# A chunked state-space scan: step sums as products of 18 rounded rows, part of VectorE's work given to ScalarE and GpSimd

## The reference, cut to what matters

```python
xdt = x * dt[..., None]
a_cum = jnp.cumsum(dt * a.reshape(G, R), axis=2)
seg = a_cum[:, :, :, None] - a_cum[:, :, None]
decay_ls = jnp.exp(jnp.where(causal, seg, -jnp.inf))
cb = jnp.einsum("bclgn,bcsgn->bclsg", cm, bm)
y_diag = jnp.einsum("bclsg,bclsgr,bcsgrp->bclgrp", cb, decay_ls, xdt)
decay_to_end = jnp.exp(a_cum[:, :, -1:] - a_cum)
states = jnp.einsum("bclgn,bclgr,bclgrp->bcgrpn", bm, decay_to_end, xdt)
chunk_decay = jnp.exp(a_cum[:, :, -1])
# h <- h * chunk_decay + states, chunk after chunk; y_off = C h exp(a_cum)
y = y_diag + y_off + x * d_skip
```

## Time and profile before

| | us |
|---|---|
| median of 3 runs | 2749.34 |
| lowest, highest | 2748.38, 2751.9 |
| the profiled execution, whole | 2747.44 |
| its span in the profile | 2745.6 |
| TensorE busy, share of the span | 2606.7, 95% |
| VectorE busy | 1770.6, 64% |
| GpSimd busy | 1586.4, 58% |
| ScalarE busy | 1311.5, 48% |

### The profile page before, as it was taken

How to read it: one execution, slowest core, us unless ns; L and a number is a source line. 1 busy time by engine, 2 the same in 40 slices (tenths; PEclk the granted TensorE clock), 3 DMA queues, 4 the chain that set the end, 5 groups by cost and what they waited for, 6 DMA issues and landing times. The chain is left out here.

```text
span 2745.6 us, 41086 instructions
## 1 busy us (share of the span) xinstructions
PE 2606.7 (95%) x14122; PEld 1834.4 (67%) x14122; DVE 1770.6 (64%) x2152; ACT 1311.5 (48%) x2072; POOL 1586.4 (58%) x1222
## 2 busy tenths in 40 slices
PE   5999999989999999799989999999999999599998
PEld 3788777767888888566645555555555555388887
DVE  5532565644214554299969888898888889555554
ACT  4433333434333333211158777787778777322221
POOL 5876666688777777478746565665666666000000
PEclk7999999999999999899979999999999999799999
DMA  2543323323333323244541212303122111333231
GB/s 104 154 157 111 124 86 132 116 89 129 128 123 138 123 99 132 70 115 131 148 135 55 71 49 61 93 24 93 55 62 78 40 40 58 123 119 107 76 113 40
DMA packets 202405, 267.95 MB, mean 98 GB/s; under 512 B 12833, under 2 KB 136033, under 8 KB 195569
## 3 DMA queue, kind: packets, MB, share of 16 engines
q1 hardware_dynamic: 202224, 265.64, 30.4%
HBM read 168.84 MB, written 96.76 MB: 97 GB/s over the span
## 5 line engine op out<-in xcount | busy, mean ns | idle before, releaser
L1969 POOL TENSOR_TENSOR a_w<-a_beta,a_rest 128x1024 f32<-128x1024 f32 (+2 forms) x320 | 560.3, 1751 | 354.0 <-DVE a_rest L1926 207.3
L763 POOL TENSOR_TENSOR f_l_lo<-f_wst,f_l_hi 128x512 fp32r<-128x512 f32 x312 | 405.0, 1301 | 269.1 <-ACT f_l_hi L631 268.8
L1926 DVE TENSOR_TENSOR_SCAN a_rest<-a_keep,a_rest,a_ones 128x513 f32<-128x513 f32 x384 | 470.0, 1262 | 10.8 <-ACT a_keep L1896 10.8
L1846 PE MATMUL a_turn<-a_ident,a_w 128*128 128x128 f32 (+1 forms) x2432 | 342.9, 279 | 7.3 <-DVE a_wt L1880 6.1
L1861 PE MATMUL a_o<-a_wt,a_v 128*64 128x512 f32 (+3 forms) x1408 | 339.4, 560 | 8.9 <-DVE a_out L1936 8.9
L499 PE MATMUL f_xz<-f_t_hi,f_l_hi 128*128 128x512 f32 x832 | 330.2, 397 | 6.9 <-issue 4.4
L499 PE MATMUL f_xz<-f_t_hi,f_l_lo 128*128 128x512 f32 x832 | 326.3, 392 | 0.0
L499 PE MATMUL f_xz<-f_t_lo,f_l_hi 128*128 128x512 f32 x832 | 326.0, 392 | 0.0
L1880 ACT COPY a_wt<-a_turn 128x512 f32<-128x512 f32 (+3 forms) x440 | 225.1, 528 | 207.0 <-PE a_turn L1846 205.5
L1846 PEld LDWEIGHTS a_turn<-a_ident,a_w 128*128 128x128 f32 (+1 forms) x2432 | 256.7, 140 | 91.5 <-issue 65.8
L1896 ACT ACTIVATE a_keep<-a_z 128x1024 f32<-128x1024 f32 (+4 forms) x352 | 300.1, 852 | 4.6 <-PE a_z L1829 4.5
(11 more groups left out here) (242 smaller groups left out, 4472.7 us busy)
## 6 DMA issues: line engine op xcount, KB each, us to landing
f_wst<-in_w_pairs SPq DMA_DIRECT2D x52, 1024.0 KB, 5.5
scratch_gate<-f_out SPq DMA_DIRECT2D x64, 256.0 KB, 2.2
o_g<-scratch_mixed SPq DMA_DIRECT2D x32, 512.0 KB, 5.5
s_xc<-scratch_xbc SPq DMA_DIRECT2D x16, 768.0 KB, 5.3
scratch_xbc<-f_out SPq DMA_DIRECT2D x36, 256.0 KB, 2.1
scratch_q_hi<-f_out SPq DMA_DIRECT2D x32, 256.0 KB, 3.5
scratch_q_lo<-f_out SPq DMA_DIRECT2D x32, 256.0 KB, 3.6
scratch_v<-f_out SPq DMA_DIRECT2D x32, 256.0 KB, 2.3
```

The source lines that it names most:

```text
L763: return nc.gpsimd.tensor_tensor(out, a, b, op).then_inc(done, 1)
L1846: mm = nc.tensor.transpose(turn[h][0:rows, qi * P:(qi + 1) * P], tile[:, h, x:x + rows], ident[:, :])
L1926: mm = nc.vector.tensor_tensor_scan(rest[r % RS][:, h, tn - 1::-1], top, ones[:, 0:1].to_broadcast([P, tn]), start, ALU.mult, ALU.min)
L1969: nc.gpsimd.tensor_tensor(w[r % AS][:, :, 0:tn], beta[r % KEEPS][:, :, 0:tn], rest[r % RS][:, :, 1:tn + 1], ALU.mult).then_inc(w_ready, 1)
```

## The change

The running sums of the decay steps are computed once, in `scan_start`: for each of the 16 chunks and 16 heads the sum up to each frame, split into a rounded high part and a rounded rest, stored to a new scratch array `cum`. The differences of two running sums are then a product over 18 rows: 16 rows hold minus the sums against ones at the place of the head (`own`), 2 rows hold ones against the sums. The rows come by three small DMAs for each unit (`load_spans`: 8 KB, and twice 4 KB), the operands are float32r. ScalarE takes `Relu` of minus the difference and then `Exp` of minus that, two passes over 128x1024 in place of one; the triangle of ones is no longer needed there. The exponentials of the three sums for all chunks (`sums`) are computed once in `scan_start`. GpSimd no longer makes `ua`; it makes `xde` (`to_end`) and fades the state (`fade`), which VectorE did. VectorE's `xdt` now waits for `xde` of two units before, its addition to the state for GpSimd's `fade`. SyncE issues the six span loads of a chunk ahead of the store of its group 0. In `scan_start` SyncE issues the stores of `cum` ahead of `scan.loads`, for which it waits for the sums, and twelve span loads behind them.

```diff
+SPANS = 2 * HPG + 2
...
+        self.sums = self.sbuf("s_sums", [P, 3, NT, HEADS])
+        self.lag = [[self.sbuf(f"s_lag{s}{g}", [SPANS, P], F32R) for g in range(GROUPS)] for s in range(2)]
+        self.rise = [[self.sbuf(f"s_rise{s}{g}", [SPANS, HPG, P], F32R) for g in range(GROUPS)] for s in range(2)]
+        self.rise_loaded = [self.sems(f"s_rise_loaded{s}", GROUPS) for s in range(2)]
...
+    def load_spans(self, sp, s, g, i):
+        steps = self.scratch["cum"][:, bass.ds(i * 2 + s, 1), g * HPG:(g + 1) * HPG, :]
+        sp.dma_start(self.rise[s][g][SPANS - 2:SPANS, :, :].bitcast(F32),
+                     steps.rearrange("q o h l -> q (o h) l")).then_inc(self.rise_loaded[s][g], 16)
+        for q in range(2):
+            sp.dma_start(self.lag[s][g][q * HPG:(q + 1) * HPG, :].bitcast(F32),
+                         steps[q, :, :, :].rearrange("o h l -> (o h) l")).then_inc(self.rise_loaded[s][g], 16)
...
+            sp.wait_ge(cum_high, START + 2)
+            sp.wait_ge(cum_low, START + 2)
+            for q in range(2):
+                for b in range(2):
+                    sp.dma_start(scratch["cum"][q, b * (NT // 2):(b + 1) * (NT // 2), :, :].rearrange("t h l -> (t h) l"),
+                                 by_step[q][b][:, :].bitcast(F32)).then_inc(cum_stored, 16)
             scan.loads(sp)
+            sp.wait_ge(lag_ones, START + 2 * GROUPS)
+            sp.wait_ge(own_kept, START + 2 * GROUPS)
+            sp.wait_ge(cum_stored, START + 64)
+            for s in range(2):
+                for g in range(GROUPS):
+                    scan.load_spans(sp, s, g, 0)
...
+            scan.constants(pool)
+            nc.gpsimd.memset(own[:, :, :], 0.0).then_inc(own_step, 1)
+            for q in range(2):
+                pool.wait_ge(own_step, START + q + 1)
+                nc.gpsimd.affine_select(out=own[:, :, :], in_=own[:, :, :], compare_op=ALU.not_equal, fill=-1.0,
+                                        base=-q * HPG, pattern=[[-1, HPG], [0, P]], channel_multiplier=1).then_inc(own_step, 1)
...
+            pe.wait_ge(scan.made, 4)
+            pe.wait_ge(steps_ready, START + 1)
+            for b in range(2):
+                last = nc.tensor.matmul(ps[:, b, 0:P],
+                                        steps[:, b * (NT // 2):(b + 1) * (NT // 2), :].rearrange("p t h -> p (t h)"),
+                                        scan.upper[:, :], start=True, stop=True)
+            last.then_inc(cum_done, 1)
+            for q, lhs in enumerate((scan.upper, scan.later, scan.ones)):
+                last = nc.tensor.matmul(psums[:, q, :], lhs[:, :], steps[:, :, :].rearrange("p t h -> p (t h)"),
+                                        start=True, stop=True)
+            last.then_inc(sums_done, 1)
...
+            act.wait_ge(cum_done, START + 1)
+            for b in range(2):
+                nc.scalar.activation(by_step[0][b][:, :], ps[:, b, 0:P], ACT.Copy).then_inc(cum_high, 1)
+            act.wait_ge(sums_done, START + 1)
+            nc.scalar.activation(scan.sums[:, :, :, :].rearrange("p q t h -> p q (t h)"), psums[:, 0:3, :],
+                                 ACT.Exp).then_inc(sums_ready, 1)
+            act.wait_ge(own_step, START + 3)
+            for s in range(2):
+                for g in range(GROUPS):
+                    nc.scalar.activation(scan.rise[s][g][0:2 * HPG, :, :], own[:, :, :], ACT.Copy).then_inc(own_kept, 1)
...
+            nc.vector.tensor_copy(steps[:, :, :], dt_tok[:, 1:NT + 1, 1, :]).then_inc(steps_ready, 1)
+            for s in range(2):
+                for g in range(GROUPS):
+                    nc.vector.memset(scan.lag[s][g][:, :].bitcast(F32), 1.0).then_inc(lag_ones, 1)
+            for b in range(2):
+                dve.wait_ge(cum_high, START + b + 1)
+                nc.vector.tensor_tensor(by_step[1][b][:, :], ps[:, b, 0:P], by_step[0][b][:, :].bitcast(F32),
+                                        ALU.subtract).then_inc(cum_low, 1)
...
+                    if more:
+                        for g in range(GROUPS):
+                            sp.wait_ge(seg_ready[s][g], i + 1 + START)
+                            scan.load_spans(sp, s, g, i + 1)
...
-            def spread_steps(s, g, i):
-
-                pool.wait_ge(seg_ready[1 - s][g], i + s + START)
-                nc.gpsimd.tensor_tensor(ua[g][:, :, :], upper[:, :].unsqueeze(1).to_broadcast([P, HPG, P]),
-                                        over_heads(dt_of(i, s, 1, g), P), ALU.mult).then_inc(ua_ready[s][g], 1)
+            def to_end(s, g, i):
+
+                hs = slice(g * HPG, (g + 1) * HPG)
+                pool.wait_ge(xdt_ready[s][g], i + 1 + START)
+                pool.wait_ge(st_done[1 - s][g], i + s + START)
+                nc.gpsimd.tensor_tensor(heads(xde[g]), heads(xdt[g]), over_heads(sums_of(i, s, 1, hs), HEAD),
+                                        ALU.mult).then_inc(xde_ready[s][g], 1)
+
+            def fade(s, g, i):
+
+                hs = slice(g * HPG, (g + 1) * HPG)
+                pool.wait_ge(off_done[s][g], i + 1 + START)
+                own = state[:, g, :].rearrange("p (h c) -> p h c", h=HPG)
+                nc.gpsimd.tensor_tensor(own, own, over_heads(sums_of(i, s, 2, hs), HEAD), ALU.mult).then_inc(decayed[s][g], 1)
...
-            pipeline(pool, (2, spread_steps), (1, skip), (-1, gate))
+            pipeline(pool, (1, to_end), (0, fade), (1, skip), (-1, gate))
...
-                    pe.wait_ge(expo_ready[1 - s], i + s + START)
-                    for n, lhs in enumerate((upper, later, ones)):
-                        rhs = (dt_tok[:, 1 + 2 * i + s, 1, :] if isinstance(i, int) else
-                               dt_tok[:, bass.ds(i * 2 + (1 + s), 1), 1, :].rearrange("p o h -> p (o h)"))
-                        last = nc.tensor.matmul(pc[:, n, :], lhs[:, :], rhs, start=True, stop=True)
-                    last.then_inc(sums_ready[s], 1)
...
-                pe.wait_ge(ua_ready[s][g], i + 1 + START)
-                pe.wait_ge(decay_ready[ps][pg], count + START)
+                pe.wait_ge(scan.rise_loaded[s][g], i * 48 + 48 + START)
+                pe.wait_ge(span_ready[ps][pg], count + START)
                 for half in range(2):
                     hs = slice(half * (HPG // 2), (half + 1) * (HPG // 2))
-                    last = nc.tensor.matmul(pseg[:, hs, :], later[:, :], ua[g][:, hs, :], start=True, stop=True)
+                    last = nc.tensor.matmul(pseg[:, hs, :], scan.lag[s][g][:, :], scan.rise[s][g][:, hs, :], start=True, stop=True)
...
-                    act.wait_ge(sums_ready[s], i + 1 + START)
-                    act.wait_ge(decayed[s][1], i + START)
-                    nc.scalar.activation(expo[s][:, :, :], pc[:, :, :], ACT.Exp).then_inc(expo_ready[s], 1)
                 act.wait_ge(seg_ready[s][g], i + 1 + START)
                 act.wait_ge(m_ready[1 - s][g], i + s + START)
-                nc.scalar.activation(decay[g][:, :, :], pseg[:, :, :], ACT.Exp).then_inc(decay_ready[s][g], 1)
+                nc.scalar.activation(decay[g][:, :, :], pseg[:, :, :], ACT.Relu, scale=-1.0).then_inc(span_ready[s][g], 1)
+                act.wait_ge(span_ready[s][g], i + 1 + START)
+                nc.scalar.activation(decay[g][:, :, :], decay[g][:, :, :], ACT.Exp, scale=-1.0).then_inc(decay_ready[s][g], 1)
...
+                dve.wait_ge(xde_ready[1 - s][g], i + s + START)
                 nc.vector.tensor_tensor(heads(xdt[g]), px[:, :, :].rearrange("p b (h c) -> p (b h) c", h=2),
                                         over_heads(dt_of(i, s, 0, g), HEAD), ALU.mult).then_inc(xdt_ready[s][g], 1)
-                dve.wait_ge(xdt_ready[s][g], i + 1 + START)
-                dve.wait_ge(expo_ready[s], i + 1 + START)
-                dve.wait_ge(st_done[1 - s][g], i + s + START)
-                nc.vector.tensor_tensor(heads(xde[g]), heads(xdt[g]), over_heads(expo[s][:, 1, hs], HEAD),
-                                        ALU.mult).then_inc(xde_ready[s][g], 1)
...
-                nc.vector.tensor_tensor(heads(yo[g]), heads(pyo), over_heads(expo[s][:, 0, hs], HEAD),
+                nc.vector.tensor_tensor(heads(yo[g]), heads(pyo), over_heads(sums_of(i, s, 0, hs), HEAD),
                                         ALU.mult).then_inc(yo_ready[s][g], 1)
-                own = state[:, g, :].rearrange("p (h c) -> p h c", h=HPG)
-                nc.vector.tensor_tensor(own, own, over_heads(expo[s][:, 2, hs], HEAD), ALU.mult).then_inc(decayed[s][g], 1)
                 dve.wait_ge(decayed[s][g], i + 1 + START)
                 dve.wait_ge(st_done[s][g], i + 1 + START)
...
```

More of the change, by code:

```diff
@@ L1269, in _ @@
                                     pattern=[[-1, META]], channel_multiplier=1).then_inc(ready, 1)
-            scan.constants(pool)
             attention.constants(pool)
@@ L1335, in scan_stage @@
         pbc = m.psum("s_pbc", [P, 2 * GROUPS, P])
-        pc = m.psum("s_pc", [P, 3, HEADS])
         pseg = m.psum("s_pseg", [P, HPG, P])
```

(4 more changed lines are left out.)

23 lines of the change are left out of this document (14 added, 9 removed).

## The result

The changed kernel takes 2772.47 us (median of 4 runs, 2769.02 to 2779.27); the kernel before, run beside it, 2748.86 (4 runs, 2747.76 to 2751.9). The ratio is 1.0087, with a 95% interval of 1.0064 to 1.0110 (intervals of ratios stand in square brackets from here on): slower, by 23.6 us, where 2759 in a range from 2743 to 2775 was forecast. The profiled execution took 2769.02 us with a span of 2767.3, against 2747.4 and 2745.6 before. Its mean granted clock is 0.963 against 0.973, and VectorE is busy 1714.5 us instead of 1770.6: the work did leave VectorE, 56 us of it, and the time rose all the same.

What follows compares the result with a forecast made beforehand. VectorE, TensorE and the ring through GpSimd's gate, store and load were taken as level bounds. 2747.4 + 2.5 + 6.5 - 2.6 - 2.4 + 6.5 = 2757.9 us, plus 1 for the median: 2759, range 2743 to 2775.

Steps and rivals of the forecast that it cites:

- the ring through store and load: Scan chunk: `front`, VectorE, GpSimd's gate, store, load, next `front`; 7.68 + 6.32 = 14.00 us, level with VectorE and TensorE.
- The steady chunk: Scan's 13 chunks: gate ends at T + 7.75, chunk 14.07 us against 13.88; +2.5 us, between -9 and +9.
- The second pass of ScalarE, and six more loads a chunk: Scan chunk: about 1.03 us more on ScalarE and 3 us of SyncE issues, both hidden.
- The start: `scan_start`: SyncE's loads wait for sums and stores, span loads end at 1157.5; +6.5 us, between +4 and +9.
- The first chunks and the end: Scan's head without `ua` and full `pseg`: -2.6 us; attention stage's loads issued earlier, last gates closer: -2.4 us.
- The clock: Scan: TensorE's holes halve its clock in about half of the chunks, 1.0 us each; +6.5 us (0 to +25).
- the likeliest case: Whole kernel: slower, clock falling in some chunks, 2759 us, alone 2754 to 2768; chance 0.42.
- The median: Whole kernel: 1 us added to the profiled execution's 2757.9 to give the median of 2759.
- the clock holds: Rival, scan's TensorE: no harmful holes, clock stays up, 2752 us, no measurable change; chance 0.28.
- VectorE was the bound, 2717: Rival, scan chunk: ring has slack, chunk falls to 10.2 to 11.6 us, total 2717 us; chance 0.04.
- The ring shortens: Rival, scan chunk: `mt` avoids `gated`, which keeps 1.27 us; chunk 13.2, total 2740 to 2745 us; chance 0.13.
- The last one: Rival, scan: clock falls in every chunk or SyncE is late, 2 us a chunk more, 2775 to 2785; chance 0.13.

Runs made afterwards that it cites:

- Opening the ring alone: Kernel before with the load of the next `xc` issued ahead of the store of group 0 on SyncE: 2746.48 us, ratio 0.9993.
- fillers: Changed kernel with ten unused 128x128 products on TensorE ahead of its wait for each chunk's `xc`: 2757.3 us, ratio 1.0031.
- the run with only the new segment sums: Changed kernel with both state operations (`xde` and the fading) moved back from GpSimd to VectorE: 2751.96 us, ratio 1.0009.
- the exchanged version: Changed kernel with the load of the next `xc` issued ahead of the store of group 0 on SyncE: 2720.47 us, ratio 0.9898.

## Why the prediction was right, and where its size was off

- **What bounds the kernel**: right. VectorE, TensorE and the ring through store and load are level. Opening the ring alone gives 0.2 us a chunk, taking work from the engines alone gives nothing, both together take the chunk from 13.88 to 11.5 us in the mean.
- **The steady chunk**: right, and to the step. Each start lay within 0.06 us of the timeline and the gate's end within 0.15, `to_end` and `fade` took 1.04 us, and 14.08 us was measured with the clock held by fillers, against 14.07. One thing in it was taken as a rule that isn't one: that GpSimd is what `mt` stretches. That held because `mt` begins first (last section). The rule of the Trainium skill (GPSIMD Engine Reference, Engine selection) of twice VectorE's time, by which 1.22 us and a chunk of 14.4 would have come out, isn't borne out at this size: 1.04 is 1.7 times half of `mt`'s 1.22. Against the same operations on VectorE, in the run with only the new segment sums, it is less still: `xde` takes 0.69 us there, and the fading 1.20, more than GpSimd's 1.04. Here the row was the better guide.
- **The second pass of ScalarE, and six more loads a chunk**: hidden, as said. No table was loaded between `Relu` and `Exp`, which take 1.02 and 1.06 us, as the Trainium skill (ScalarE: Activation LUTs, Table sets) has it. The span loads take about 2.4 us of SyncE a chunk with the time between them, where 3 had been forecast, and by the timelines are issued before the gate ends.
- **The start**: +5.2 of +6.5 us. The twelve span loads took 3.8 us, 0.25 to 0.31 each, where 0.46 had been taken from the row of another load. The first load began where the forecast had it, 5.55 us into the stage.
- **The first chunks and the end**: -2.1 of -2.6, and -2.4 of -2.4. The second agrees by luck. Counted from the end of the 13 chunks the attention stage's first load is issued 2.6 us earlier than before, not 1.2, and the last two gates stand 3.17 us apart instead of 2.47, where they were forecast to be 1.2 closer.
- **The clock**: the mechanism was right, the term mis-sized. The +6.5, in about half of the chunks 1.0 us each, was 16 to 17.4 us, with 9 of 13 chunks 1.1 to 2.7 us longer than 14.08. Two errors are in it. The smaller is the count, 9 and not 6.5. The larger is the price. The step said that `pyo` would come later than `to_end` by so much that such a chunk loses 1.0 us; it priced the half speed of B, C and `px` (0.65, measured 0.63), but not in full what follows through `pseg`, the turning of `ysum` and `pyo` itself, all ahead of the fade on TensorE. At half clock `pyo` ends at T + 6.1, not T + 3.4, and `fade` and `gated` come 2.7 us later with it (T + 10.58 against T + 7.90 for the gate's end). Doubling all of TensorE's queue up to `pyo` would have given it: the same rows, one more step. With 2.7 us for a chunk that is slow from its first product and fewer for one in which the fall comes later, half of the chunks would have cost some 13 us, and the forecast would have stood at 2765, an estimate made after the result. That the measured median lies inside the range, 2.5 us under its upper end, is due to the range's allowance of 1.5 us more for each chunk and not to the likeliest case.
- **The median** lay 3.5 us above the profiled execution, where 1 was allowed. The four runs scatter by 10 us, those of the exchanged version by 5. That the falls of the clock are the cause isn't shown: with the clock held by fillers seven runs still scatter by 8.
- **Of the rivals**, "the clock holds" is the run with fillers less their own price. "VectorE was the bound, 2717" is wrong for this kernel, which has the ring, but its figure is close to what the kernel gives once the ring is open (2720), and its chunk of 11.6 us to the 11.36 to 11.75 seen there. "The ring shortens" fell: `mt` ran right beside `gated`, which took 2.25 us in most chunks. In four, where `mt` was late, `gated` did keep its 1.27, but those are chunks at half clock. The last one, with its 2 us a chunk, is the nearest in size to what happened; the measured median lies 2.5 us below its lower end. TensorE's own work had been put at 10.2 us a chunk, which doesn't follow from the prediction's own terms; it is 11.2: 13.78 less 2.3 for `pseg` and what `pc` took. The hole of 1.1 us forecast for the middle of a chunk is 0.29 in the chunk at full clock. Neither changed the sum.

Open: whether the fall of the clock follows the hole at the chunk's head alone or the light work around it as well (fewer fillers, or fillers elsewhere, were not tried), why two of the loads take 6.5 us to land, and what of the 11.4 us in the exchanged version is TensorE's (no run took work from it).

## What to carry to other kernels

If several engines are busy for 97% of the time, look for the ring that is as long as they are: follow the last operation of an iteration through its store and the load that is queued behind it to the first operation of the next. Work taken from a full engine is worth nothing while that ring stands, and less than nothing when it lands on the engine inside the ring; issue the load ahead of the store first, then move the work. And an engine freed of work stands idle somewhere: price the clock that it then gets for every product up to the one that the ring waits for.

## What the hardware showed that was not expected

- Holes of 2.37 to 3.79 us at a chunk's head brought the half clock in nine cases of nine (0.45 of 2.90 us busy, then 0.50 for 6.80 us). Behind shorter ones it can go either way: with only the fading back on VectorE the unit behind a hole of 1.00 to 1.34 us in the middle of a chunk had its `pyo` at 1.91 or 1.92 us in all but two chunks, and the two at full clock had holes of 1.34 and 1.32. Ten products for nothing in each hole at a chunk's head kept the clock at 1.00 throughout.
- Where `mt` on VectorE and `gated` on GpSimd, both with all operands in SBUF, overlap, the one that begins second pays. Alone they take 1.22 and 1.27 us. With `mt` first by 0.32 us, `gated` takes 2.26 and `mt`, which still meets the end of `xd`, 1.44. With `gated` first by 0.34 and by 0.07, in chunks at half clock, it keeps its 1.27 and `mt` takes 2.01 and 2.27. The second of each pair is longer by 0.8 to 1.05 us, about what the first had left. The first of these pairs with `gated` ahead, from the kernel after:

```profile
1194.80 2.01 DVE L1611 TENSOR_TENSOR s_mt<-s_decay,s_cbm 128x1024 f32<-128x1024 f32 x1
...
1194.46 1.27 POOL L1518 TENSOR_TENSOR s_gated<-s_yt,s_zt 128x512 f32<-128x512 f32 x1
```

- Beside VectorE's reads of PSUM GpSimd's operations keep their 1.04 us.
- Moving four stores behind the loads on SyncE's queue hid a wait of 3.3 us and opened one of 3.4 us, their landing.
